# A hybrid decoder layer: input norms from token-major copies of x and the memory, reciprocals spread by a product

## What is computed

```python
def rmsnorm(x, g):
    xf = x.astype(jnp.float32)
    y = xf * lax.rsqrt(jnp.mean(xf * xf, axis=-1, keepdims=True) + EPS)
    return (y * g.astype(jnp.float32)).astype(x.dtype)
...
    kv = rmsnorm(mem, g_mem) @ w_mem_kv
...
    h = rmsnorm(x, g_pre_mix)
    proj = h @ w_in
```

## Time and profile before

| | us |
|---|---|
| median of 3 runs | 2011.98 (2010.7 to 2014.7) |
| the profiled execution | 2014.58 |
| its span, first to last instruction | 2012.8 |
| PE busy | 1957.8 (97%) |
| DVE, ACT, POOL busy | 903.7, 621.5, 896.5 |
| mean granted clock of TensorE | 0.989 |
| mem_in, 1024 KB: issue to landing | 5.0 |
| x_in, 1376 KB each, 3 loads: median | 8.5 |
| w_raw, 512 KB each, 113 loads: median | 3.7 |

### The profile page before, as it was taken

The page is one execution under the profiler, slowest core; times in us unless marked ns, Lnnn a source line. Parts: engine busy times, 40 slices in busy tenths (PEclk is TensorE's granted clock), DMA queues, the critical chain, the costliest instruction groups (busy, mean ns, idle before and its releaser), DMA issues.

```text
span 2012.8 us, 33480 instructions
## 1 busy us (share of the span) xinstructions
PE 1957.8 (97%) x13077; PEld 1908.2 (95%) x13077; DVE 903.7 (45%) x1966; ACT 621.5 (31%) x1184; POOL 896.5 (45%) x533
## 2 busy tenths in 40 slices
...
GB/s 190 105 43 85 136 110 43 43 115 141 74 53 58 136 136 43 43 89 141 225 175 147 123 158 129 137 46 124 124 88 125 77 211 87 103 85 105 147 53 85
DMA packets 89289, 218.22 MB, mean 108 GB/s; under 512 B 7721, under 2 KB 40745, under 8 KB 88793
## 3 DMA queue, kind: packets, MB, share of 16 engines
q1 hardware_dynamic: 78784, 192.48, 28.6%
...
## 4 chain that ended last, share of the span: by engine, by line
PE 88%; DVE 5%; issue 2%; ACT 2%; POOL 2%; DMA 0%; DVEq 0%; SPq 0%; ACTq 0%; POOLq 0%
PE bank L892 78%; PE bank L1041 1%; PE bank L1044 1%; PE bank L1235 1%; PE bank L1033 1%; PE bank L996 1%; PE bank L1039 1%; PE bank L1133 1%; POOL w_lo L698 1%; DMA w_raw<-w_stream 0%; ACT P_sb L1437 0%; POOL h_lo L713 0%; DVE acc L2074 0%; DVE gates L2071 0%; DVE acc L1763 0%
## 5 line engine op out<-in xcount | busy, mean ns | idle before, releaser
L892 PE MATMUL bank<-h_hi,w_hi 128*128 128x344 f32 (+1 forms) x2048 | 651.1, 318 | 2.4 <-POOL w_lo L698 2.2
L892 PE MATMUL bank<-h_lo,w_hi 128*128 128x344 f32 (+1 forms) x2048 | 637.7, 311 | 0.0
L892 PE MATMUL bank<-h_hi,w_lo 128*128 128x344 f32 (+1 forms) x2048 | 636.0, 311 | 0.0
L702 POOL TENSOR_TENSOR w_hi<-w_raw,ones 128x1024 fp32r<-128x1024 f32 x77 | 147.4, 1914 | 628.1 <-PE bank L892 628.1
L892 PEld LDWEIGHTS bank<-h_hi,w_hi 128*128 128x128 f32 x2048 | 387.4, 189 | 7.1 <-issue 3.5
L892 PEld LDWEIGHTS bank<-h_hi,w_lo 128*128 128x128 f32 x2048 | 387.2, 189 | 0.9
L892 PEld LDWEIGHTS bank<-h_lo,w_hi 128*128 128x128 f32 x2048 | 387.1, 189 | 0.0
L704 POOL TENSOR_TENSOR w_lo<-w_raw,w_hi 128x1024 fp32r<-128x1024 f32 x77 | 185.7, 2412 | 6.1
L2241 DVE TENSOR_TENSOR acc<-acc,bank 128x344 f32<-128x344 f32 x72 | 36.9, 513 | 292.0 <-PE bank L892 292.0
L1268 ACT ACTIVATE side_t<-bank 128x344 f32<-128x344 f32 x96 | 44.0, 459 | 284.3 <-PE bank L892 284.3
L1763 DVE SCALAR_TENSOR_TENSOR acc<-acc,rstd 128x258 f32<-128x258 f32 x128 | 126.7, 1032 | 0.1
...
## 6 DMA issues: line engine op xcount, KB each, us to landing
w_raw<-w_stream SPq DMA_DIRECT2D x113, 512.0 KB, 3.7
...
```

Of the source, the lines that this page charges most:

```text
L702: pool.tensor_tensor(w_hi[:, slot, :], w_raw[:, slot, :], ones[:, 0:1].to_broadcast([P, 1024]), ALU.mult).then_inc(s_hi_made, 1)
L892: last = pe.matmul(out, st, mv, start=i == 0, stop=i == n - 1)
```

## The change

The memory and x are loaded a second time, token-major: mem_tok as 128 x 2 x 1024 into xt_c, x_tok as 86 x 12 x 1024 (1032 = 12 x 86) in six loads of two blocks each, into xt_a and xt_b in turn. A token's features then lie in one row, and ACT squares the row and adds it up in one instruction (a block of 86 tokens of x each, four for a group; two of the first group's and one of the memory's two are DVE's). The root and the reciprocal are taken of columns, two for the memory and four for a group of x. `diagonal` puts each column on the diagonal of an 86 x 86 (or 128 x 128) block, and one product with ones spreads it to all partitions. The memory is no longer scaled: ACT makes m_hi with the weight of the norm as a scale, DVE m_lo, and the 1/root goes onto the results of the memory's products as DVE drains them (`mem_take`). POOL has four h_lo of eight, DVE four. The gate slab is loaded in its 36 used columns of each block. All loads are ordered anew on SP, and a load into xt_a or xt_b waits for the squares of what was in it.

```diff
-X_POOL = 5
+X_POOL = 4
+B86 = 86
...
+            sp.dma_start(vec[:, :], vecs).then_inc(s_mem_loaded, 16)
+            sp.dma_start(bif[:, :], b_if).then_inc(s_mem_loaded, 16)
+            sp.dma_start(m0[:, :], stm).then_inc(s_mem_loaded, 16)
             sp.dma_start(mem_in[:, :, :], memT).then_inc(s_mem_loaded, 16)
-            sp.dma_start(vec[:, :], vecs).then_inc(s_const_loaded, 16)
-            sp.dma_start(bif[:, :], b_if).then_inc(s_const_loaded, 16)
-            sp.dma_start(m0[:, :], stm).then_inc(s_const_loaded, 16)
-            sp.dma_start(x_in[:, :, tok[0]], xT[:, :, tok[0]]).then_inc(s_x_loaded[0], 16)
             slab(1, 1, None)
-            slab(0, 0, None)
-            sp.dma_start(x_in[:, :, tok[1]], xT[:, :, tok[1]]).then_inc(s_x_loaded[1], 16)
+            sp.dma_start(w_raw[:, 0, :].rearrange("p (k c) -> p k c", k=KD)[:, :, 0:GATES],
+                         w_stream[0].rearrange("p (k c) -> p k c", k=KD)[:, :, 0:GATES]).then_inc(s_slab_loaded[0], 16)
+            sp.dma_start(xt_c[:, :, :], mem_tok).then_inc(s_memt_loaded, 16)
+
+            def tok_load(g, e):
+                if g:
+                    sp.wait_ge(s_tok_sq_act, (0, 2 + e, 5 + 2 * e)[g])
+                    sp.wait_ge(s_tok_sq_dve, 2 + e if g == 1 else 3)
+                sp.dma_start(xt[e][0:B86, :, :], x_tok[:, 4 * g + 2 * e:4 * g + 2 * e + 2, :])\
+                    .then_inc(s_tok_loaded[e], 16)
+
+            def x_load(g):
+                sp.dma_start(x_in[:, :, tok[g]], xT[:, :, tok[g]]).then_inc(s_x_loaded[g], 16)
+            tok_load(0, 0)
+            tok_load(0, 1)
             slab(2, 0, 1)
-            sp.dma_start(x_in[:, :, tok[2]], xT[:, :, tok[2]]).then_inc(s_x_loaded[2], 16)
-            for n in range(3, SLAB_HEAD + 2):
+            x_load(0)
+            slab(3, 1, 2)
+            tok_load(1, 0)
+            tok_load(1, 1)
+            x_load(1)
+            tok_load(2, 0)
+            tok_load(2, 1)
+            x_load(2)
+            for n in range(4, SLAB_HEAD + 2):
...
-            for e in range(4):
-                pool.wait_ge(s_mem_hi, e + 1)
-                pool.tensor_tensor(m_lo[:, 2 * e:2 * e + 2, :], mem_in[:, 2 * e:2 * e + 2, :],
-                                   m_hi[:, 2 * e:2 * e + 2, :].bitcast(F32), ALU.subtract).then_inc(s_mem_norm, 1)
             for n in range(2, SLAB_HEAD + 2):
-                if n in (3, 5, 7):
-                    x_lo((n - 3) // 2)
+                if n in (4, 5, 6):
...
-            for k in range(KD):
-                if k % 2 == 0:
-                    pe.wait_ge(s_mem_norm, k // 2 + 1)
-                last = pe.matmul(b_U[:, 0:MEM], ones[:, :], mem_sq[:, k, :], start=k == 0, stop=k == 7)
-            last.then_inc(s_mem_norm, 1)
-
-            def x_sum(g):
-                for k in range(KD):
-                    i = g * KD + k
-                    pe.wait_ge(s_x_sq, i + 1)
-                    pe.matmul((b_S, b_W, b_N)[g][:, 0:G], ones[:, :], sq_ring(i % 6), start=k == 0, stop=k == 7)\
-                        .then_inc(s_x_sq_used, 1)
+
+            def mem_spread():
+                pe.wait_ge(s_mem_norm, 11)
+                pe.matmul(b_N[:, 0:MEM], ones[:, :], rstd0[:, 0:MEM], start=True, stop=True).then_inc(s_mem_norm, 1)
+
+            def x_spread(g):
+                pe.wait_ge(s_x_std, 3 * g + 2)
+                if g == 2:
+                    pe.wait_ge(s_mem_norm, 13)
+                pe.matmul((b_S, b_W, b_N)[g][:, 0:G], ones[0:B86, :], rstd0b[0:B86, tok[g]], start=True, stop=True)\
+                    .then_inc(s_x_std, 1)
...
-            x_sum(0)
-            x_sum(1)
-            pe.wait_ge(s_mem_norm, 10)
+            pe.wait_ge(s_mem_norm, 9)
             mem_product(0)
+            mem_spread()
             mem_product(1)
-            x_sum(2)
+            x_spread(0)
+            mem_product(2)
+            x_spread(1)
             pe.wait_ge(s_slab_split, SLAB_GATE + 1)
-            for g in range(NG):
-                gates_of(g)
-                mem_product(2 * g + 2)
-                mem_product(2 * g + 3)
+            gates_of(0)
+            mem_product(3)
+            x_spread(2)
+            gates_of(1)
+            mem_product(4)
+            mem_product(5)
+            gates_of(2)
+            mem_product(6)
+            mem_product(7)
...
+            def x_squares(g, js):
+                for j in js:
+                    act.wait_ge(*xt_load(g, j))
+                    t = xt[j // 2][0:B86, j % 2, :]
+                    act.activation(t, t, ACT.Square,
+                                   accum_out=nrm[0:B86, 2 + 4 * g + j:3 + 4 * g + j]).then_inc(s_tok_sq_act, 1)
 
             def x_std(g):
-                act.wait_ge(s_x_sq_used, KD * (g + 1))
-                act.activation(rstd0b[:, tok[g]], (b_S, b_W, b_N)[g][:, 0:G], ACT.Sqrt, scale=1.0 / D, bias=eps[:, 0:1]).then_inc(s_x_std, 1)
+                act.wait_ge(s_tok_sq_act, tok_act(g))
+                act.wait_ge(s_tok_sq_dve, tok_dve(g))
+                r = nrm[0:B86, 2 + 4 * g:6 + 4 * g]
+                act.activation(r, r, ACT.Sqrt, scale=1.0 / D, bias=eps[0:B86, 0:1]).then_inc(s_x_std, 1)
...
+                act.wait_ge(s_mem_loaded, 64)
+                for k in range(KD):
+                    act.activation(m_hi[:, k, :], mem_in[:, k, :], ACT.Copy, scale=vec[:, V_MEM + k:V_MEM + k + 1])\
+                       .then_inc(s_mem_norm, 1)
+
+            def m_square():
+                act.wait_ge(s_memt_loaded, 16)
+                act.activation(xt_c[:, 0, :], xt_c[:, 0, :], ACT.Square, accum_out=nrm[:, 0:1]).then_inc(s_tok_sq_act, 1)
+
+            def m_std():
+                act.wait_ge(s_mem_norm, 9)
+                act.wait_ge(s_tok_sq_act, 1)
+                act.wait_ge(s_tok_sq_dve, 1)
+                act.activation(nrm[:, 0:2], nrm[:, 0:2], ACT.Sqrt, scale=1.0 / D, bias=eps[:, 0:1]).then_inc(s_mem_norm, 1)
+
+            def m_rows():
+                act.wait_ge(s_mem_norm, 12)
+                act.activation(mem_std[:, :], b_N[:, 0:MEM], ACT.Copy).then_inc(s_mem_norm, 1)
...
-            m_squares()
-            act.wait_ge(s_mem_norm, 5)
-            act.activation(mem_std[:, :], b_U[:, 0:MEM], ACT.Sqrt, scale=1.0 / D, bias=eps[:, 0:1]).then_inc(s_mem_norm, 1)
-            x_squares(0, range(KD))
             m_high()
+            m_square()
+            m_std()
+            x_squares(0, (0, 2))
+            m_rows()
             x_std(0)
-            x_squares(1, range(KD))
             slab_hi(2)
+            slab_hi(3)
+            x_hi(0)
+            x_squares(1, range(4))
             x_std(1)
-            x_hi(0)
-            slab_hi(3)
-            x_squares(2, range(KD))
-            mem_taken(0)
+            slab_hi(4)
+            x_hi(1)
+            x_squares(2, range(4))
             x_std(2)
-            slab_hi(4)
-            mem_taken(1)
-            x_hi(1)
             slab_hi(5)
-            mem_taken(2)
-            slab_hi(6)
-            mem_taken(3)
             x_hi(2)
-            for n in (4, 5, 6):
-                slab_hi(n + 3)
-                mem_taken(n)
+            for n in range(6, 10):
+                slab_hi(n)
...
+            def diagonal(out, rows, col, n):
+                r = nrm[0:rows, col:col + n]
+                step(dve.reciprocal(r, r))
+                return dve.tensor_tensor(out.rearrange("p (j t) -> p j t", j=n),
+                                         ident[0:rows, 0:rows].unsqueeze(1).to_broadcast([rows, n, rows]),
+                                         r.unsqueeze(2).to_broadcast([rows, n, rows]), ALU.mult)
+
+            def mem_take(n):
+                dve.wait_ge(s_mem_norm, 13)
+                dve.wait_ge(s_mem_ready, n + 1)
+                dve.tensor_tensor(kvT[:, n, :], (b_I, b_U)[n % 2][:, 0:MEM], mem_std[:, :], ALU.mult).then_inc(s_mem_taken, 1)
...
+            dve.wait_ge(s_memt_loaded, 16)
+            token_square(xt_c[:, 1, :], P, 1)
+            dve.wait_ge(s_mem_norm, 10)
+            diagonal(rstd0[:, 0:MEM], P, 0, 2).then_inc(s_mem_norm, 1)
+            for j in (1, 3):
+                dve.wait_ge(*xt_load(0, j))
+                token_square(xt[j // 2][0:B86, 1, :], B86, 2 + j)
+            mem_take(0)
+            x_diagonal(0)
+            mem_take(1)
+            x_scale(0)
+            x_low(0)
+            mem_take(2)
+            x_diagonal(1)
+            x_scale(1)
+            x_low(1)
+            mem_take(3)
+            x_diagonal(2)
+            x_scale(2)
+            x_low(2)
+            gate_rows(0)
+            gate_rows(1)
+            mem_take(4)
+            mem_take(5)
+            gate_rows(2)
+            mem_take(6)
+            mem_take(7)
...
+        "x_tok": x.reshape(12, B86, D).transpose(1, 0, 2),
+        "mem_tok": inputs["mem_prompt"][0].reshape(2, P, D).transpose(1, 0, 2),
```

(40 more changed lines are left out.)

42 lines of the change are left out of this document (22 added, 20 removed).

## The result

The changed kernel takes **2098.47 us** (median of 4 runs, 2097.36 to 2100.2), the kernel before beside it 2013.34 (4 runs, 2010.7 to 2014.96): 1.0423 times the time, 95% interval 1.041 to 1.0436, slower. The forecast was 2091.6, with a range of 2081 to 2112. The time was lost ahead of F, the start of head 0's first unit, which moved from 64.72 us to 149.95.

The account below looks back on a forecast made before the run. TensorE bounds the kernel, so F's shift counts: slab 4 at 109.9, plus 32 and 2.4 for the clock, gives 144.3 against 64.72, 79.6 later. 2014.6 + 79.6 = 2094.2, less 2.6 for the median: 2091.6 us, range 2081 to 2112.

Parts of the forecast that it names:

- Two engines: x_tok loads: 86 rows go in equal shares to 2 DMA engines, 43 rows each, 13.5 us a load; chance 0.84.
- The sum up to slab 4: What the two DMA engines must move until slab 4 lands: 109.9 us, of which six x_tok loads 81.3.
- the bound above, 20 us from the mean over queue 1: Upper end of the range: 8192 bytes at queue 1's mean price, 0.39 us, make x_tok's loads 20 us longer.
- 32 us from slab 4 to F: From slab 4's landing, through squares, spreading, POOL's splits and memory products, to head 0's first unit: 32 us.
- The clock: TensorE before F: idling some 30 us lowers the granted clock to 0.50; 2.4 us lost, bounds 0 to 10.
- After F: Gate chain behind F: Ln ends 5.7 us and o_h's drain starts 24.4 us after F; 2.7 us cover, no cost.
- m_lo on DVE: Eight m_lo at the start, DVE: 0.40 us each, done near 11 us.
- Rival 1: x_tok's 86 rows spread over all 16 engines: slab 4 near 45 us, F 77, 2024 us; chance 0.11.
- Rival 2: Rows spread and slab 4, landing before 33 us, delays nothing: 9.3 us gained, 2002.7 us; chance 0.03.
- the first product moves 9.3 us earlier, all that can be gained: First memory product on TensorE: starts near 15.2 us instead of 24.49, the most the change can gain.

Follow-up runs that it names:

- e1: Changed kernel with each x_tok load cut into one of 80 rows and one of 6; 2031.22 us, 1.009 times the kernel before.
- e5: Changed kernel with each x_tok load cut into one of 84 rows and one of 2; 2033.86 us.
- e2: Changed kernel with each x_tok load cut into two of 43 rows; 2179.89 us.
- e6: Changed kernel with the three x_in loads issued ahead of the first x_tok load; 2090.98 us, 1.0391 times the kernel before.
- e9: e7 with the first memory product ahead of the first group's sum, slab 4's high part ahead of the third group's squares, last gates moved; 2023.44 us.
- e4: Changed kernel with x_tok loads cut 80 + 6, the start reordered and five h_lo on POOL; 2024.29 us, 1.0059 times the kernel before.
- e7: Kernel before with only the change's memory scaling, cut gate slab and earlier slab 2, no token-major loads; 2016.12 us, 1.0016 times the kernel before.
- e12: Kernel before with fp32r one-pass norm sums, cut gate slab, slabs 1 and 2 loaded earlier, slab 2's high part earlier on ACT; 2008.31 us, 0.9977 times.
- e10: e9 with the norms' sums made in one pass (squares and ones in fp32r); 2021.26 us, 1.0038 times the kernel before.

## Why the prediction was right, point by point

**Two engines.** The step on which all rests held: shares of 0.12 to 0.13 with 52 GB/s, e1, e5 and e2.

**The sum up to slab 4** said 109.9 and was 117.95. Its largest term, six x_tok loads at 13.5 = 81.3 us, was mis-sized. The landings, where ACT begins or DVE's wait ends, are 27.98, 41.92, 64.20 and 77.60; the loads took 16.6, 13.9 and 29.85 for the second pair. The third pair took 31.9, from x_in's 81.18 to 116.68 - 3.6. Together 92.3, 11.0 more. One load of each pair was worked off beside the 14 other engines' x_in, where a packet is dearer (e6). The price came from stores with nothing beside them; the bound above, 20 us from the mean over queue 1, was the term that covered it, by its size and not by its cause. Against it x_in took 10.8 rather than 12.6, slabs 3.5 rather than 4.2, and the first part, up to mem_tok at 11.39, 0.4 less: 109.9 + 11.0 - 2.9 = 118.0. The last pair was issued at 66.41 and 79.81 rather than 62 and 75, and still before the two engines had run dry.

**32 us from slab 4 to F** held, by other parts: the squares ended a little sooner, POOL had slab 5 only after them (127.64), and was through with slab 6 18.5 us after slab 4 rather than 19.1; then 9.7 us of TensorE, 1.1 and 2.4. That these differences cancel to nothing is luck.

**The clock** was granted at 0.50 from 90.5 to 124.6 us and 1.00 after. The term of 2.4 us cost nothing: of TensorE's work only memory product 3 ran in it, and it was drained from 126.14 on, when ACT's last square had ended at 126.13. The cover was nil; in e6, with the squares out earlier, the same product did lie on the path. So F came 8.05 us later than said from slab 4's sum, less the 2.4 of this term: 5.65 us, 149.95 against 144.3. Two errors with opposite signs made the forecast look closer than its largest term was.

**After F** the cover held. Ln ended at 154.55, 4.6 us after F (5.7 said), DVE's drain of o_h began at 173.21, 23.3 us after (24.4 said). 1948.45 us from F to the end is what it was.

**m_lo on DVE** was priced at 0.40 us, from a row whose second input is a bank. This one reads two tiles in SBUF, beside POOL (least, median, most ns; then POOL's timeline):

```profile
L1798 DVE SCALAR_TENSOR_TENSOR m_lo<-mem_in,vec,m_hi x8: 476/746/2555, 7.6 to 13.1; 128x256 fp32r<-128x256 f32 x8
...
10.86 2.07 POOL L736 TENSOR_TENSOR w_hi<-w_raw,ones 128x1024 fp32r<-128x1024 f32 x1
13.01 2.40 POOL L738 TENSOR_TENSOR w_lo<-w_raw,w_hi 128x1024 fp32r<-128x1024 f32 x1
```

The first ran in 0.48 us ahead of POOL's start at 8.95, the last took 2.56 us beside POOL's 2.40. All eight took 8.05 us, not 3.2. Here it delayed the first product by under 1 us, since POOL's split of slab 1 ended at 15.41 anyway. In e9 it is the h_lo of the second group, not m_lo, that stand beside POOL on the chain (6.41 us). The Trainium skill ("SBUF — State Buffer", section "Who interferes with whom") says that an instruction of VectorE with two SBUF inputs contends with one of GpSimd that reads SBUF, for ports that are locked by one of them at a time. The trace agrees: the last m_lo began with POOL's instruction of 2.40 us and ended at 15.69, 0.3 us after it.

**Rival 1**'s mechanism, rows spread over all engines, did not hold for 86 rows; e1 shows what it would have given: F 85.72 against the 77 said for it. Cut well, the change would have cost 18 us, for slab 4 came at 53.14 rather than 45. **Rival 2**'s condition, slab 4 before 33 us, was nearly met in e4 (35.78), and F was still 76.2. It counted slab 4 alone, where x_tok's last load landed at 49.4 us.

The prediction's reading of the start was one-sided: "the first product moves 9.3 us earlier, all that can be gained" took that for a gain in F. In e7, which has the memory's part alone, the first product started 4.4 us earlier and F came 3.8 later. e7 to e12 show that TensorE's and POOL's rows up to F are full within a few us of each other, and DVE's too once it has the memory's low parts and drains (e9, e10); a start earlier on one is waited away on the next.
